# Gated linear attention in a hybrid block: one projection and a states stage become two passes over the tokens, by columns

## The reference

```
qg, kg, vg, og, lr, ... = split(h @ w_in)        # 256, 256, 512, 512, 32 columns of h (1024 wide)
gk = log_sigmoid(lr @ w_gk2 + b_gk2) / 16        # per direction, head (4) and key dimension (64)
# per head, in chunks of 64 tokens, forward and backward:
b   = cumsum(gk)                                  # within the chunk
q_t = q * exp(b); k_t = k * exp(-b); k_e = k * exp(b_last - b)
o_intra = tril(q_t @ k_t.T) @ v
u   = k_e.T @ v;  decay = exp(b_last);  state = decay * state + u
o   = o_intra + q_t @ state_before
out = rms_norm(o_f + o_b, gla_g) * silu(og)
```

## Time and profile before

| | |
|---|---|
| median of 3 runs | 3918.46 us (3915.69 to 3920.26) |
| the profiled execution | 3915.24 us; its span in the trace 3913.7 us |
| mean granted TensorE clock | 0.94 |
| busy share | PE 91%, DVE 50%, ACT 40%, POOL 27% |
| projection stage | starts at 1255.86 us, 336.82 us long |
| states stage | starts at 1592.68 us, 234.52 us long |
| outputs stage | starts at 1827.20 us, 164.64 us long |

### The profile page before, as it was taken

How to read it: one execution, slowest core, us unless ns; L and a number is a source line. 1 busy time by engine, 2 the same in 40 slices (tenths; PEclk the granted TensorE clock), 3 DMA queues, 4 the chain that set the end, 5 groups by cost and what they waited for, 6 DMA issues and landing times. The chain is left out here.

```text
span 3913.7 us, 49412 instructions
## 1 busy us (share of the span) xinstructions
PE 3551.4 (91%) x17922; PEld 2925.0 (75%) x17922; DVE 1968.8 (50%) x2948; ACT 1582.2 (40%) x2216; POOL 1046.8 (27%) x606
## 2 busy tenths in 40 slices
PE   5786999999997999787869799999999999999998
PEld 2674777777775999566758678888888888888897
DVE  2765888888885111244843333333333332433364
ACT  2442788888886111374224422222222222222233
POOL 0553999999995000011211100000000000000000
PEclk8997999999997999666989999999999999999999
DMA  4232111111102222223544553334334333433374
GB/s 166 103 116 82 39 44 43 44 40 44 43 22 78 81 71 82 70 88 111 161 144 172 177 156 96 113 119 128 97 113 143 97 101 110 145 96 102 103 209 150
DMA packets 375236, 400.97 MB, mean 102 GB/s; under 512 B 37588, under 2 KB 282548, under 8 KB 375092
## 3 DMA queue, kind: packets, MB, share of 16 engines
q1 hardware_dynamic: 358888, 358.26, 29.4%
q0 software_dynamic: 8432, 31.46, 2.1%
q10 hardware_dynamic: 7776, 9.44, 0.7%
HBM read 318.02 MB, written 81.08 MB: 102 GB/s over the span
## 5 line engine op out<-in xcount | busy, mean ns | idle before, releaser
L790 POOL TENSOR_TENSOR att_tlo<-att_prob,att_thi 128x1024 fp32r<-128x1024 f32 x292 | 692.9, 2397 | 113.2 <-ACT att_thi L959 113.2
L331 PE MATMUL ff_p<-ff_hhi,ff_whi 128*128 128x512 f32 (+1 forms) x1760 | 649.9, 369 | 35.3 <-DVE ff_hlo L2037 22.9
L1981 ACT ACTIVATE ff_whi<-ff_ws 128x2048 fp32r<-128x2048 f32 (+1 forms) x170 | 317.5, 1868 | 901.2 <-PE ff_p L333 884.4
L332 PE MATMUL ff_p<-ff_hlo,ff_whi 128*128 128x512 f32 (+1 forms) x1760 | 649.3, 369 | 0.0
L333 PE MATMUL ff_p<-ff_hhi,ff_wlo 128*128 128x512 f32 (+1 forms) x1760 | 649.2, 369 | 0.0
L1985 DVE TENSOR_TENSOR ff_wlo<-ff_ws,ff_whi 128x2048 fp32r<-128x2048 f32 (+1 forms) x170 | 378.4, 2226 | 386.0 <-ACT ff_whi L1981 385.7
L1927 POOL TENSOR_TENSOR ff_rs<-ff_ms,neg_half 128x1 f32<-128x1 f32 x18 | 9.9, 552 | 1594.7 <-DVE ff_ms L2057 1594.7
L331 PEld LDWEIGHTS ff_p<-ff_hhi,ff_whi 128*128 128x128 f32 x1760 | 333.5, 189 | 92.1 <-issue 37.5
L954 ACT ACTIVATE att_prob<-att_p_s 128x512 f32<-128x512 f32 x584 | 337.6, 593 | 118.6 <-PE att_p_s L850 117.7
L1002 DVE TENSOR_REDUCE att_mx<-att_p_r 128x1 f32<-128x512 f32 x512 | 343.6, 683 | 72.8 <-PE att_p_r L814 72.8
L332 PEld LDWEIGHTS ff_p<-ff_hlo,ff_whi 128*128 128x128 f32 x1760 | 333.4, 189 | 55.4
(11 more groups left out here) (242 smaller groups left out, 6211.0 us busy)
## 6 DMA issues: line engine op xcount, KB each, us to landing
ff_ws<-in_w_ffn_dram SPq DMA_DIRECT2D x320, 512.0 KB, 4.7
att_aw<-in_ada_w_dram SPq DMA_DIRECT2D x8, 2048.0 KB, 8.2
proj_d<-gp_out SPq DMA_DIRECT2D x18, 784.0 KB, 4.0
hT_d<-qkv_hT SPq DMA_DIRECT2D x18, 512.0 KB, 2.8
qT_d<-qkv_qT SPq DMA_DIRECT2D x18, 512.0 KB, 2.7
att_qa<-qT_d SPq DMA_DIRECT2D x36, 256.0 KB, 2.8
gp_h<-hT_d SPq DMA_DIRECT2D x18, 512.0 KB, 4.9
qkT_d<-gs_qkT SPq DMA_DIRECT2D x18, 512.0 KB, 2.9
```

The source lines that it names most:

```text
L331: pe.matmul(out, ah, bh, start=first, stop=False)
L332: pe.matmul(out, ah, bl, start=False, stop=False)
L790: pool.tensor_tensor(tlo[:, sl, :], prob[:, sl, :], thi[:, sl, :].bitcast(F32), ALU.subtract).then_inc(s.lo, 1)
L1981: act.activation(whi[:, par, 0:cols], ws[:, par, 0:cols], ACT.Copy).then_inc(s.w_hi, 1)
```

## The change

The projection is cut by columns, and each part takes over a piece of the states stage:

- `gla_keys` (names ga_) projects q, k and lr, 544 columns in two banks of 272, so 48 matmuls of 272 columns a tile. The gate chain of the same tiles, three steps behind, is woven into the step, up to the store of qkT_d. q, k and lr are taken from SBUF (four buffers `qk`), not from HBM. ke is stored to HBM (`ke_d`). Every second step loads and splits one row block of the weights of v and og (`wv`).
- `gla_values` (gb_) projects v and og, 1024 columns in two banks of 512, 48 matmuls of 512 columns a tile. Between the two banks PE makes `u` of the tile before, and DVE and ACT update the states. Silu of og and the product with the gain are made here, and v and that product gg are stored.
- `gla_outputs` loads v and gg in place of v and og, and no longer makes Silu and gg.
- The loops of these three stages are written out over all tiles (`tiles`). There is no proj_d.

More of the change, by code:

```diff
@@ L1085, in gla_projection @@
         lo = ph.sb("lo", [P, 2, KC, P], F32R)
[L1086 to L1170, removed]
@@ L1173, in slot_of @@
[L1173 to L1188, removed]
+        qk = ph.sb("qk", [P, BUFS, DA])
@@ L1227, in _, with weights @@
[L1227 to L1231, removed]
+                def weights():
+                    for k in range(KC):
+                        wait(sp, s.w_lo, k - W_STAGES + 1)
+                        rows = slice(k * P, (k + 1) * P)
+                        sp.dma_start(stage[:, k % W_STAGES, 0:NG], g.w_in[0, rows, 0:NG]).then_inc(s.w[k % W_STAGES], 16)
+                        sp.dma_start(stage[:, k % W_STAGES, NG:DA], g.w_in[0, rows, LR0:D_GLA]).then_inc(s.w[k % W_STAGES], 16)
@@ L1244, in step @@
                         sp.dma_start(g.qkT_tile(t), qkT[:, par].rearrange("p h a q -> p (h a q)")).then_inc(s.out[par], 16)
-                steps(sp, 5, step)
-                sp.wait_ge(s.out0, 16 * (NT // 2))
-                sp.wait_ge(s.out1, 16 * (NT // 2))
-                sp.wait_ge(s.scan, 2 * GH * NT)
-                sp.dma_start(g.new_f.rearrange("h k v -> k h v"), g.states[0:DK, slot_of(T_CTX // CH, True)]).then_inc(s.fin, 16)
-                sp.wait_ge(s.fin, 16)
+                tiles(6, step)
+                for par in range(2):
+                    sp.wait_ge(s.out[par], 16 * (NT // 2))
+                    sp.wait_ge(s.ko[par], 16 * (NT // 2))
             @block.gpsimd
@@ L1299, in step @@
                         wait(pe, s.etq, t)
[L1300 to L1301 removed]
+                        for n in range(GH):
+                            last = pe.transpose(p_q[:, n * P:(n + 1) * P], qt[:, n].rearrange("p r d -> p (r d)"), g.ident[:, :])
                         last.then_inc(s.tq, 1)
@@ L1310, in step @@
-                        wait(pe, s.ub, t)
-                        wait(pe, s.scan, 2 * GH * t)
-                        for c in range(2):
-                            rows = slice(c * CH, (c + 1) * CH)
-                            for h in range(GH):
-                                last = pe.matmul(p_u[c][:, h * DV:(h + 1) * DV], ke[rows, h].rearrange("p r d -> p (r d)"),
-                                                 vin[rows, par, h * DV:(h + 1) * DV], start=True, stop=True)
-                        last.then_inc(s.u, 1)
+                    if T := U.at(3):
+                        t, hf, par = T
+                        pe.wait_ge(s.e1, t + 1)
+                        wait(pe, s.edec, t - 1)
+                        wait(pe, s.lrT, t)
+                        pe.transpose(p_a[0:2 * LR, 0:P], qk[:, t % BUFS, NG:DA], g.ident[:, :]).then_inc(s.lrp, 1)
@@ new lines, in step @@
+                        act.wait_ge(s.h[par], (hf + 1) * 16)
+                        wait(act, s.b1, t - 1)
+                        act.activation(hi[:, par], h[:, par], ACT.Copy).then_inc(s.hi, 1)
+                    if u == 1:
+                        for k in range(KC):
+                            act.wait_ge(s.w[k % W_STAGES], 32 * (k // W_STAGES + 1))
+                            act.activation(w_hi[:, k, :], stage[:, k % W_STAGES, :], ACT.Copy).then_inc(s.w_hi, 1)
+                    k = value_weight(u - 1)
@@ new lines, in step @@
+                        wait(dve, s.tk, t)
+                        dve.tensor_tensor(kt[:, :, :, :], bc(k_of(t), 2, 2), e2[:, :, :, :], ALU.mult).then_inc(s.kt, 1)
+                    if T := U.at(1):
+                        t, hf, par = T
+                        dve.wait_ge(s.hi, t + 1)
+                        wait(dve, s.b1, t - 1)
+                        dve.tensor_tensor(lo[:, par], h[:, par], hi[:, par].bitcast(F32), ALU.subtract).then_inc(s.split, 1)
+                    if u == 1:
+                        for k in range(KC):
+                            dve.wait_ge(s.w_hi, k + 1)
+                            dve.tensor_tensor(w_lo[:, k, :], stage[:, k % W_STAGES, :], w_hi[:, k, :].bitcast(F32), ALU.subtract).then_inc(s.w_lo, 1)
@@ L1562, in step @@
                         last.then_inc(s.o, 1)
-                steps(pe, 4, step)
+                tiles(4, step)
             @block.scalar
             def _(act):
-                def step(U):
+                def step(U, u):
                     if T := U.at(2):
@@ L1584, in step @@
                         act.activation(mT[:, par, :], p_m[:, :], ACT.Copy).then_inc(s.et, 1)
-                steps(act, 4, step)
+                tiles(4, step)
             @block.vector
@@ L1632, in step @@
                         backwards(chunk + 1, ctx, behind - 1)
-                steps(dve, 4, step)
+                tiles(4, step)
                 backwards(0, True, scans_behind(NT - 1))
```

448 lines of the change are left out of this document (286 added, 162 removed).

## The result

The changed kernel takes 3892.46 us (median of 4 runs, 3883.96 to 3897.68), the kernel before 3917.07 (4 runs beside them). The ratio is 0.9935 with a 95% interval of 0.9915 to 0.9955: faster, but by 25 us where 78 were forecast, and outside the range. The profiled execution is the fastest of the four, 3883.96 us with a span of 3882.4, so its stages add up to a gain of 31.7 us where the medians differ by 25.

The account below looks back on a forecast made before the run. Bounds: TensorE for the projection, a ring of waits for states, VectorE for outputs. 736.0 - 262.5 - 244 - (164.6 - 13) = 78 us off 3915.2 gives 3837, plus 3.2: 3840 us; 3810 to 3872 holds 8 in 10.

Parts of the forecast that it names:

- VectorE and POOL have more room: In the gla_keys step: these two engines have more slack than ScalarE, whose work adds up to some 9.5 us a step.
- max(11.8, 11.2): gla_keys step without clock drops: the longer of the dependency cycle, 11.8 us, and TensorE's own work, 11.2 us.
- The ring: gla_keys cycle: p_g to gate 5.81 us, handover 0.2, cumulative sums 1.84, chunk sums 0.92, one bank 3.04; together 11.8.
- SP's loads: gla_keys: next h load queues behind the qkT copies' wait, is wanted 12 us later, lands in under 5; no cost.
- what PE does counts, not only that it does something: TensorE's clock in gla_keys: the kind of work, not only idling, lowers it, so drops were expected despite 0.6 us idle.
- one drop of the clock in two steps: gla_keys: a fall to 1.2 GHz every second step, costing 1.75 us each, makes the step 11.8 + 0.9 = 12.7 us.
- The stretch of the states stage: 20 us in the old states stage with PE busy 18.55 at clock 0.50, cited against the rule that idling lowers it.
- the rival of a clock that sinks into the states stage's: gla_keys: a drop hits the chain and slows the next bank; steps of 14 to 17.8 us, 3860 to 3917; chance 0.18.
- the things came by which the prediction says it would be wrong: gla_keys clock below 0.8, PE waiting for copies or loads, 272-column matmuls clearly over 0.127 us, or outputs' tiles at 8.2.
- the long state update: gla_outputs: one update takes 1.37 us against 0.352 median, beside POOL's gg; removing gg saves 1.02 us a tile.
- TensorE's 6.81 and its drops: gla_outputs: PE's 6.81 us a tile is the next bound, each clock drop adds up to 1.5 us; gain taken 0.75.
- The copies on ScalarE: gla_keys: two copies ahead of Abs end about 1 us before p_g; no cost if the step is not under 11 us.

Follow-up runs that it names:

- the first experiment: The changed kernel with two buffers each for qt and kt instead of one: 3806.29 us, ratio to before 0.9721.
- The kernel with the step mended: Changed kernel with two qt/kt buffers, or VectorE's qs, qt, kt behind lrT, or TensorE's qt/kt transposes at step head: 3806.29, 3805.01, 3803.2 us.

## Why the prediction was wrong

The step that failed is "VectorE and POOL have more room", in the sum of the keys step. The busy time bears it out, VectorE is busy for 60 of 220 us there. The order of its stream does not. So the step was forecast at max(11.8, 11.2), and 12.7 with the drops, and measured at 16.4. The ring was added up as a chain of results: p_g, Abs, Exp, Ln, mn, gate, cumulative sums. The release of a buffer was not in it, though the prediction did so for SP's loads. The transposes stand at the end of TensorE's step in the rows of the change, so the numbers were at hand in the trace of the kernel before: the queue from transpose to gate costs 0.69 + 0.68 + 1.22 + 0.68 + 0.69 less overlaps = 3.8 us. Added to TensorE's 10.7 that is over 14, before the clock.

A second step failed the other way: "what PE does counts, not only that it does something", and with it one drop of the clock in two steps. Without the long wait there was none in 170 us, with the same work (the first experiment), and none in the steps whose wait was filled. TensorE: Matmul & The Clock Gate, HAM oscillation, of the Trainium skill, which puts the fall down to waits in which the engine idles, would have given the right answer; both agree with it. The stretch of the states stage on which I relied, 18.55 us busy of 20 at 0.50, says that the clock stayed low in such work, not that the work brought it down: at the lower clock p_g took 2.07 us in place of 1.12, so the same work fills more of the time. What brought it down in that stage was not tried. So the rival of a clock that sinks into the states stage's comes near in time (3860 to 3917 holds the result, and 14 to 17.8 the step) by luck: it names the wrong cause, and the clock was the consequence.

None of the things came by which the prediction says it would be wrong: the stage's clock was 0.83 and not below 0.8, TensorE waited for the gate, the matmuls of 272 columns and the outputs' tiles were as short as forecast. What gave it away was the length of that wait, 3.8 us in place of 0.6.

Point by point:

- The ring without that wait was right. In the first experiment p_g starts at 1386.43, the next cumulative sums at 1392.30, 5.87 us (forecast 5.81 + 0.2), and from cumulative sums to p_g 5.84 (forecast 5.80). Sum 11.7, forecast 11.8; idle time 0.56, forecast 0.6. The mean over all steps is 11.55, since half of them split no weights.
- Matmuls of 272 columns: 0.125 us apart, forecast 0.1266.
- The head of `gla_keys`: p_g at 28.9 us, forecast 31; cumulative sums at 34.9, forecast 37.
- `gla_values`, mechanism right and size off: u takes 1.16 us and a step 12.2, forecast 1.71 and 12.8. 18 x 0.6 = 11 is all of the difference of 10. The 1.71 was read rightly, at a clock of 1.00 and with no wait inside, but it is the price of another order, which the prediction passed over. Before, the four matmuls of the first chunk (rows 0 to 63) stood ahead of the four of the second (rows 64 to 127); after, the chunks alternate. Of the sixteen passes in the trace before, most start one at a time, 0.11 us apart; after, all start in pairs, the two of a pair 6 to 7 ns apart, and mostly one pair every 0.11 us. The order was not tried by itself.

```diff
-                        for c in range(2):
-                            rows = slice(c * CH, (c + 1) * CH)
-                            for h in range(GH):
-                                last = pe.matmul(p_u[c][:, h * DV:(h + 1) * DV], ke[rows, h].rearrange("p r d -> p (r d)"),
...
+                        for n in range(GH):
+                            for c in range(2):
+                                rows = slice(c * CH, (c + 1) * CH)
+                                last = pe.matmul(p_u[c][:, n * DV:(n + 1) * DV], ke[rows, par, n].rearrange("p r d -> p (r d)"),
```

- `gla_outputs`: the long state update is gone, as forecast, and what the GPSIMD Engine Reference, Specifications, of the Trainium skill says of the shared SBUF interface agrees with the runs: 1.0 us a tile by experiment, 1.02 by the row. I took only 0.75, for fear of TensorE's 6.81 and its drops. A tile takes 6.86. That it is near 6.81 is chance: TensorE still waits 1.0 us a tile, and VectorE, whose only wait in a tile is 1.1 us for POOL's root, sets the pace. The drops didn't come: the stage's clock is 0.94, against 0.87.
- The copies on ScalarE and SP's loads cost nothing in the changed kernel, as forecast; once the wait and p_g's place are mended, TensorE is busy for 140 us of 140 beside them.

The kernel with the step mended (3803 to 3806) is 109 to 112 us faster than before, more than the 78 forecast: the drops, u and the outputs were each put too high.

## What to carry to other kernels

Add up a software pipeline's ring with the releases of its buffers in it, not only the results: for each buffer with one copy ask who frees it, where that stands in the other engine's order, and what is queued behind the wait. A mean busy share of 27% doesn't show that an engine is free when it is wanted. And where TensorE waits some microseconds once a step and its clock is low, take the wait away first; here the clock came back by itself.

## What was not expected of the hardware

- Fillers pay. 30 useless matmuls of 256 columns a step, 3.83 us, in a wait of 3.4 to 4.5 us made the stage 31 us shorter.
- The fall of the clock doesn't mark the wait that caused it: in the step shown it reads 1.00 through 4 us of idle time and falls 0.2 us after work starts again; in the other steps with a projection and such a wait it falls between 1.2 us ahead of that start and 1.1 behind it.
- 4.7 us of transposes, cumulative sums, chunk sums and p_g in a row (1379.44 to 1384.15 in the kernel with p_g moved), once in every step of 10.66, leave it at 1.00 when nothing idles.
